# Another address for the second homes of the activation buffers, another order of the first modulation chunks, and the output of the LRU on other engines

## The chip, the cores and the metric

The kernel runs on one core of a Trainium2 chip. The time is the device time of one execution in microseconds; lower is better. One execution on the same kind of chip was recorded with the profiler, and all rows below are from it. PE is TensorE (PEld its weight loads), DVE is VectorE, ACT is ScalarE, POOL is GpSimd, SP is SyncE, which only issues DMAs here. "Granted clock" is the share of TensorE's full clock of 2.4 GHz that the chip granted; the other level, 0.50, is 1.2 GHz.

## What is computed

Two blocks of two layers each, on 256 tokens of width 1024 (and, in the first layer alone, 256 context tokens beside them). Cut to what matters here:

```
x_lat, x_ctx = layer_norm(x), layer_norm(ctx)
for l in 0, 1:                                 # first block
    sh1, sc1, g1, sh2, sc2, g2 = split(silu(c) @ w_mod[l] + b_mod[l], 6)
    a = x * (1 + sc1) + sh1                    # sh1: columns 0..1023, sc1: 1024..2047
    m = mixer(a)                               # a @ w_in, Fourier mix, two attentions, gates, w_out
    x = layer_norm(ALPHA * x + (1 + g1) * m)
    x = layer_norm(ALPHA * x + (1 + g2) * swiglu(x * (1 + sc2) + sh2))
for i in 0, 1:                                 # second block
    h = modulate(rms_norm(x), sh, sc)
    i == 0: y = (rg_lru(conv(h @ w_in)) * gelu(h @ w_y)) @ w_out + b_out
            # rg_lru: h[t] = a[t] * h[t-1] + u[t], a scan over the tokens
    i == 1: y = pool_mixer(h)
    x = x + gate * y
    x = x + gate * (relu(h @ w1) ** 2 @ w2)    # the MLP, width 4096
return rms_norm(x)
```

## The kernel before

Everything is float32. Activations lie transposed: 128 features on the partitions, 8 tiles of features, tokens along the row. A **unit** is a product with 512 columns of weights (4 output tiles `m`, 8 inner tiles `k`). Each float32 factor is split in a high part, rounded to the matmul's format, and a low rest, and a tile product is three matmuls, high x high (L546), high x low (L547) and low x high (L548), each with its own load of 128x128 weights on PEld. A unit's weights come by DMA into the buffers `RAW`; ACT copies them to the high part `SH` (L501) and DVE subtracts to get the low part `SL` (L507), one instruction of each for each `m`, mostly while the unit before is multiplied. The loop `Unit.pe` waits for `SL` of its `m`, for the bank of PSUM, and for its input tile by tile.

**Homes.** The moving operand of these matmuls is one of three pairs of buffers: `AB` (inputs of a layer), `HH`/`HL` (hidden values), `YB` (branch values). `pair` gives `AB` and `YB` two homes in the same memory: `at(0)` begins at a multiple of 128 bytes, `at(SHIFT)` begins `SHIFT` floats further on, and `H_IN` does so for `HH` and `HL`. `SHIFT` is 48 floats, 192 bytes, so the second home begins 64 bytes behind a multiple of 128 bytes. The first home serves layer 0, in which the matmuls take 512 tokens; the second serves layer 1 and the second block, in which all but a few take 256. `Y8H` and `Y8L`, the input of the LRU's output product, lie in the second home too. The weights `SH` and `SL` and all tile steps are multiples of 128 bytes.

**Modulation chunks.** `w_mod` is read in chunks of 512 columns. Most are hosted by a unit: `Side.pe_rows` (L367) multiplies the chunk by the conditioning vectors, DVE flips the result (`flip`), four small matmuls gather it (`gather_flipped`, L324), and DVE adds the bias (`dve`). The first four chunks belong to `Opening`: two of them are the shifts of layer 0 (tiles 0 to 3, then 4 to 7), two the scales. `Opening.sp` issues XIN, the first unit's weights and then the four chunks, all on SP's queue, into `SIDE`, `EARLY1` (in the high half of `AB`), `EARLY2` (in the low half) and `EARLY3` (in `YB`). `Opening.pe` runs `rows_of` (L1769) and `turn` for all four, one behind another; `Opening.dve` has the matching `flip` (L1702) and `add` (L1707) between the statistics, the reciprocal (L1723), the splits of the first unit's weights and the centring of tiles 0 and 1 (L1033, L1067), and then makes the scales in `DER` (`prep`, L2150). Then `Norm` runs: for each tile, ACT writes X (L1091) and the modulated tile (L1110), DVE rounds it into the high part of `AB` (L1052) and subtracts for the low (L1054), and PE starts the first unit (`w_in`, by tiles: all four `m` of tile 0, then of tile 1, and so on).

**LRU.** Two units `gelu[0]`, `gelu[1]` (`w_y`) are multiplied while DVE makes the scans. `GeluLru.dve` has, in this order: the splits of `gelu[1]`'s weights 0 and 1, `scan` of tiles 0 to 3, the splits 2 and 3, `scan` of tiles 4 to 7 (GI times LT at L676, then four scans at L679). `LruOut.pool` multiplies each tile by its gate on POOL (L1818), `LruOut.dve` waits for that, rounds (L1825) and subtracts (L1827) tile by tile. The splits of `lru_w_out` come between the two halves. The unit behind, a `Residual` with `late=4`, takes input tiles 0 to 3 of its first two `m` first, then tiles 4 to 7 of them.

Of the kernel before, what the change touches and what calls it, by code (L numbers as in the profile page):

```python
# [25 lines left out]
P = 128  # L26
# [20 lines left out]
SHIFT = 48  # L47
# [77 lines left out]
class Counts:  # L125
# [30 lines left out]
    def up(self, name, by=1):  # L156
# [13 lines left out]
            "tap_done", "tile_squared"],  # L170
    "dve": ["weight_low", "dve_read", "side_summed", "side_flipped", "side_added", "dve_done", "centred", "input_low", "one_minus_a2", "scanned",
            "max_done", "probs_ready", "branch_low", "keys_copied", "hidden_low", "var_done",
            "rotary_copied", "rotated_done", "lambda_done", "diagonals", "bias_done", "latent_normed", "copied_out"],
# [7 lines left out]
def build(nc, A, out, const):  # L181
# [42 lines left out]
    def reg(name, at, shape, dt=F32):  # L224
# [43 lines left out]
    EARLY1, EARLY2, EARLY3 = (sb(f"EARLY{j + 1}", [P, KT, 512], at=at)  # L268
                              for j, at in enumerate((AH_AT, AL_AT, YH_AT)))
# [58 lines left out]
    class Side:  # L328
# [3 lines left out]
        flip_at = 3  # L332

# [36 lines left out]
        def flip(self, e, K, j):  # L370
            e.wait_ge(sem["side_rows"], K.at("side_rows", j + 1))
            e.transpose(MODROW[:, :], PS[4][:, :]).then_inc(K.up("side_flipped"), 1)
# [7 lines left out]
        def dve(self, e, K, j):  # L380
            e.wait_ge(sem["side_turned"], K.at("side_turned", j + 1))
# [65 lines left out]
    class Unit:  # L447
# [3 lines left out]
        mid = None  # L451
        kt = KT
# [50 lines left out]
        def split_dve(self, e, K, m):  # L503
            p = m // 2
            e.wait_ge(sem["weight_high"], K.at("weight_high", m + 1))
# [17 lines left out]
        def pe(self, e, K):  # L523
            waited = -1
            for m, k in self.order():
                if self.side and self.by_k and (m, k) == (0, self.rows_at):
                    self.side.pe_rows(e, K, 0)
# [117 lines left out]

    class GeluLru(Gelu):
# [25 lines left out]
        def scan(self, e, K, half):  # L672
            t = slice(4 * half, 4 * half + 4)
            e.wait_ge(sem["root_done"], K.at("root_done", 4 * half + 4))
            e.wait_ge(sem["gated_done"], K.at("gated_done", 4 * half + 4))
            e.tensor_tensor(GI[:, t, :], GI[:, t, :], LT[:, t, :], ALU.mult).then_inc(K.up("dve_done"), 1)  # L676
            e.wait_ge(sem["dve_done"], K.own("dve_done"))
            for k in range(4 * half, 4 * half + 4):
                e.tensor_tensor_scan(XC[:, k, :], LA[:, k, :], GI[:, k, :], 0.0, ALU.mult, ALU.add) \  # L679
                    .then_inc(K.up("scanned"), 1)  # L680

        def dve(self, e, K):
# [9 lines left out]
            self.scan(e, K, 0)  # L692
            for m in (2, 3):
                self.nxt.split_dve(e, K, m)
            self.scan(e, K, 1)
# [204 lines left out]
    class Norm:  # L900


# [133 lines left out]
        def dve(self, e, K):  # L1036
# [9 lines left out]
            for k in range(KT):  # L1046
                if k + 1 < KT and (k or not self.split):
                    self.centre(e, K, k + 1)
                if self.to == "a":
# [5 lines left out]
                        .then_inc(K.up("input_low"), 1)  # L1055

# [550 lines left out]
    class Opening:  # L1607
# [3 lines left out]
        ROWS = (4, 3)  # L1611
# [3 lines left out]
        def __init__(self, unit, norm):  # L1615
            self.unit, self.norm = unit, norm
            unit.loaded = True

# [6 lines left out]
        def sp(self, e, K):  # L1625
# [7 lines left out]
            for j in range(4):  # L1633
                e.dma_start(self.places[j][:, :, :], rows(wmod[0])[:, :, j * 512:(j + 1) * 512]) \
                    .then_inc(K.up(f"chunk{j}_loaded", 16), 16)
# [28 lines left out]
        def dve(self, e, K):  # L1664
# [32 lines left out]
            name, first = bmod[0]  # L1697
            t, r = place[name]

            def flip(j):  # L1700
                e.wait_ge(sem["side_rows"], K.at("side_rows", j + 1))
# [741 lines left out]
```

## Time and profile before

| | |
|---|---|
| median of 3 runs | 2149.03 us (2142.33 to 2150.68) |
| the profiled execution's own time | 2156.49 us |
| its span, first to last instruction | 2154.3 us |
| mean granted clock | 0.959 |
| PE busy | 1993.8 us, 93% |
| PEld busy | 1644.9 us, 76% |
| DVE busy | 1285.3 us, 60% |
| ACT busy | 845.8 us, 39% |
| POOL busy | 138.9 us, 6% |
| bytes read from HBM | 329.31 MB, 153 GB/s over the span |

A busy PE is not PE at its peak: a matmul's record reaches over the next one's start, so the pace is read from the starts, or from how many start in a window, not from the busy share. The layers follow each other in time: layer 0 to about 1045 us, layer 1 to 1635, the LRU layer with its MLP to 1931, and pooling with its MLP to the end.

### The profile page before, as it was taken

How to read it: one execution, taken by the hardware profiler on the slowest of the kernel's cores; microseconds unless marked ns; L12 is line 12 of the kernel's file. 1: busy time of each engine (PE TensorE's matmuls, PEld its weight loads, DVE VectorE, ACT ScalarE, POOL GpSimd, SP SyncE). 2: the span in 40 equal slices, each digit the busy share in tenths (PEclk: the TensorE clock that was granted, in tenths of full speed). 3: DMA queues.
4: the chain of work that ended last, by engine and by line, in shares of the span. 5: the costliest groups of instructions: out<-in, count | busy, mean ns of one | idle time of the engine just before them, and what ended most of it. 6: DMA issues, size and time to landing. Idle time of an engine off the chain costs nothing.

```text
span 2154.3 us, 32049 instructions
## 1 busy us (share of the span) xinstructions
PE 1993.8 (93%) x12468; PEld 1644.9 (76%) x12468; DVE 1285.3 (60%) x2184; ACT 845.8 (39%) x1364; POOL 138.9 (6%) x118
## 2 busy tenths in 40 slices
PE   4999989999999999999898989989997899988998
PEld 2776657546768788887677664879997899988998
DVE  5422464564447567777634466566667776676665
ACT  4422263263124122222433444354445644444444
POOL 0000000000030001203000000020111300000000
PEclk8999999999999999999899899999997999998999
DMA  8642513105544555546465140856652446543653
GB/s 292 215 139 78 176 40 93 49 1 186 166 159 144 189 193 195 196 156 227 120 213 172 49 133 1 274 196 196 196 195 91 145 157 191 182 155 98 196 186 127
DMA packets 280758, 332.07 MB, mean 154 GB/s; under 512 B 13190, under 2 KB 229692, under 8 KB 280508
## 3 DMA queue, kind: packets, MB, share of 16 engines
q1 hardware_dynamic: 268608, 323.05, 46.0%
q10 hardware_dynamic: 12028, 7.32, 1.3%
q8 instruction: 85, 1.39, 0.3%
q14 instruction: 37, 0.30, 0.0%
HBM read 329.31 MB, written 1.05 MB: 153 GB/s over the span
## 4 chain that ended last, share of the span: by engine, by line
PE 75%; DVE 8%; issue 5%; DMA 5%; ACT 4%; POOL 1%; SPq 1%; DVEq 0%; ACTq 0%; POOLq 0%
PE ps L546 20%; PE ps L547 19%; PE ps L548 19%; PE ps L1316 3%; DVE SL L507 2%; PE ps L1342 2%; DMA RAW<-in_w_in 2%; PE ps L367 2%; PE ps L1326 2%; PE ps L924 1%; ACT SH L501 1%; DMA RAW<-in_w_out 1%; DMA EARLY<-in_w_mod 1%; PE ps L1551 1%; DMA RAW<-in_w_branch 1%
## 5 line engine op out<-in xcount | busy, mean ns | idle before, releaser
L507 DVE TENSOR_TENSOR SL<-RAW,SH 128x1024 fp32r<-128x1024 f32 (+2 forms) x448 | 524.8, 1175 | 434.6 <-ACT SH L501 429.9
L546 PE MATMUL ps<-AB,SH 128*128 128x256 f32 (+1 forms) x1984 | 646.7, 326 | 38.8 <-DVE AB L1054 20.7
L547 PE MATMUL ps<-AB,SH 128*128 128x256 f32 (+1 forms) x1984 | 639.7, 322 | 0.0
L548 PE MATMUL ps<-AB,SL 128*128 128x256 f32 (+1 forms) x1984 | 639.0, 322 | 0.0
L501 ACT ACTIVATE SH<-RAW 128x1024 fp32r<-128x1024 f32 (+2 forms) x448 | 443.2, 997 | 439.4 <-PE ps L548 273.7
L546 PEld LDWEIGHTS ps<-AB,SH 128*128 128x128 f32 x1984 | 379.7, 191 | 90.1 <-issue 32.2
L548 PEld LDWEIGHTS ps<-AB,SL 128*128 128x128 f32 x1984 | 379.7, 191 | 29.4
L547 PEld LDWEIGHTS ps<-AB,SH 128*128 128x128 f32 x1984 | 379.2, 191 | 28.0
L546 PE MATMUL ps<-HH,SH 128*128 128x256 f32 (+1 forms) x992 | 307.0, 309 | 4.0 <-DVE HL L757 1.6
L547 PE MATMUL ps<-HL,SH 128*128 128x256 f32 (+1 forms) x992 | 304.7, 307 | 0.0
L548 PE MATMUL ps<-HH,SL 128*128 128x256 f32 (+1 forms) x992 | 304.6, 307 | 0.0
L546 PEld LDWEIGHTS ps<-HH,SH 128*128 128x128 f32 x992 | 188.0, 189 | 19.5 <-issue 4.2
L548 PEld LDWEIGHTS ps<-HH,SL 128*128 128x128 f32 x992 | 187.9, 189 | 9.8
L547 PEld LDWEIGHTS ps<-HL,SH 128*128 128x128 f32 x992 | 187.0, 189 | 9.3
L771 POOL TENSOR_TENSOR S<-X 128x512 f32<-128x512 f32 (+1 forms) x6 | 10.7, 1780 | 1462.3 <-DVE X L798 1462.3
L546 PE MATMUL ps<-YB,SH 128*128 128x256 f32 (+1 forms) x256 | 84.8, 331 | 9.1 <-DVE SL L507 6.1
L1376 ACT ACTIVATE PR<-ps,SM 128x512 f32<-128x512 f32 (+1 forms) x96 | 59.2, 616 | 62.2 <-PE ps L1326 55.8
L547 PE MATMUL ps<-YB,SH 128*128 128x256 f32 (+1 forms) x256 | 83.1, 324 | 0.0
L548 PE MATMUL ps<-YB,SL 128*128 128x256 f32 (+1 forms) x256 | 82.9, 324 | 0.0
L777 POOL TENSOR_TENSOR S<-S,SQR 128x256 f32<-128x256 f32 (+1 forms) x51 | 52.0, 1020 | 445.6 <-ACT SQR L827 445.6
L798 DVE SCALAR_TENSOR_TENSOR X<-ps,DER,X 128x256 f32<-128x256 f32 x96 | 43.1, 477 | 60.8 <-PE ps L548 60.7
L415 DVE SCALAR_TENSOR_TENSOR MODROW<-SIDE,CC,MODROW 128x512 f32<-128x512 f32 x98 | 77.5, 790 | 3.0
(283 smaller groups left out, 2188.1 us busy)
## 6 DMA issues: line engine op xcount, KB each, us to landing
SIDE<-in_w_mod SPq DMA_DIRECT2D x45, 2048.0 KB, 8.0
RAW<-in_ffn_w SPq DMA_DIRECT2D x64, 1024.0 KB, 5.4
RAW<-in_w_in SPq DMA_DIRECT2D x44, 1024.0 KB, 6.1
RAW<-in_w_ffn_gate SPq DMA_DIRECT2D x22, 1024.0 KB, 8.6
RAW<-in_w_ffn_up SPq DMA_DIRECT2D x22, 1024.0 KB, 5.4
RAW<-in_w_ffn_down SPq DMA_DIRECT2D x16, 1024.0 KB, 5.6
RAW<-in_w_branch SPq DMA_DIRECT2D x24, 512.0 KB, 3.6
RAW<-in_w_out SPq DMA_DIRECT2D x8, 1024.0 KB, 6.4
```

The costliest lines, as they stand in the source:

```text
L367: ins = e.matmul(PS[4][32 * g:32 * g + 32, :], CC[:, k, :], SIDE[:, k, :], start=k < 4, stop=k >= 4)
L415: e.scalar_tensor_tensor(out=MODROW[:, :], in0=SIDE[:, k, :], scalar=v, in1=MODROW[:, :], op0=ALU.mult, op1=ALU.add).then_inc(K.up("side_s ...
L501: e.activation(SH[:, m, 0:kt, :], RAW[p][:, 0:kt, o:o + P], ACT.Copy).then_inc(K.up("weight_high"), 1)
L507: e.tensor_tensor(SL[:, m, 0:kt, :], RAW[p][:, 0:kt, o:o + P], SH[:, m, 0:kt, :].bitcast(F32), ALU.subtract).then_inc(K.up("weight_low"), 1)
L546: e.matmul(ps, SH[:, m, k, :], xh, start=k == 0, stop=False)
L547: e.matmul(ps, SH[:, m, k, :], xl, start=False, stop=False)
L548: ins = e.matmul(ps, SL[:, m, k, :], xh, start=False, stop=k == self.kt - 1)
L777: e.tensor_tensor(S2[:, c0:c1], S2[:, c0:c1], SQR[:, t % 2, c0:c1], ALU.add).then_inc(K.up("square_added"), 1)
L798: ins = e.scalar_tensor_tensor(out=X[:, i, c:c + SEQ], in0=PS[m][:, c:c + SEQ], scalar=self.scale(s, i), in1=X[:, i, c:c + SEQ], op0=ALU.m ...
L1316: e.matmul(self.scores_of(n), q, k, start=True, stop=True).then_inc(K.up("scores_done"), 1)
L1326: ins = e.transpose(PS[self.TURNED[n % 2]][:, j * P:(j + 1) * P], PR[:, n % 2, j * P:(j + 1) * P], IDENT)
L1376: e.activation(PR[:, n % 2, 0:c1 - c0], self.scores_of(n), ACT.Exp, bias=SM[:, n % 4:n % 4 + 1], accum_out=SM[:, 4 + n % 4:5 + n % 4]).the ...
```

## The change

There are three edits. `SHIFT` becomes 56 floats, so the second homes of `AB`, `YB`, `HH` and `HL` begin 224 bytes on, 96 bytes behind a multiple of 128. The four chunks of the opening are fetched and used in the order 1, 3, 2, 4 (by first column 0, 1024, 512, 1536), the last two of them inside the first unit and its normalization; the third chunk goes to another place (`EARLY2` now in the region of the hidden buffers), the sums use bank 7 in place of bank 3. And the LRU's output is made with whole halves (128x1024) on DVE and ACT, not tile by tile on POOL and DVE, with the second scan behind `gelu[1]`'s first part.

```diff
-SHIFT = 48
+SHIFT = 56
...
-    EARLY1, EARLY2, EARLY3 = (sb(f"EARLY{j + 1}", [P, KT, 512], at=at)
-                              for j, at in enumerate((AH_AT, AL_AT, YH_AT)))
+    EARLY1, EARLY3 = (sb(f"EARLY{j}", [P, KT, 512], at=at) for j, at in ((1, AH_AT), (3, YH_AT)))
+    EARLY2 = reg("EARLY2", 2048, [P, KT, 512])
...
+    def gated_out(e, K, half):
+        t = slice(4 * half, 4 * half + 4)
+        e.tensor_tensor(XC[:, t, :], XC[:, t, :], GB[:, t, :], ALU.mult).then_inc(K.up("gated_out"), 1)
+
+    def low_out(e, K, half):
+        t = slice(4 * half, 4 * half + 4)
+        e.wait_ge(sem["out_high"], K.at("out_high", 1))
+        e.tensor_tensor(Y8L[:, t, :], XC[:, t, :], Y8H[:, t, :].bitcast(F32), ALU.subtract) \
+            .then_inc(K.up("hidden_low", 4), 4)
+
+    def high_out(e, K, half):
+        t = slice(4 * half, 4 * half + 4)
+        e.wait_ge(sem["gated_out"], K.at("gated_out", 1 - half))
+        e.activation(Y8H[:, t, :], XC[:, t, :], ACT.Copy).then_inc(K.up("out_high"), 1)
...
-        ROWS = (4, 3)
+        ROWS = (4, 7)
+        CHUNKS = (0, 2, 1, 3)
...
-            flip(0)
+            self.flip(e, K, 0)
             self.unit.split_dve(e, K, 0)
-            add(0)
+            self.unit.split_dve(e, K, 1)
+            self.flip(e, K, 1)
+            self.add(e, K, 0)
             e.wait_ge(sem["root_done"], K.at("root_done", 1))
             e.reciprocal(RSTD[:, :], VAR[:, :]).then_inc(K.up("dve_done"), 1)
-            flip(1)
-            self.unit.split_dve(e, K, 1)
-            add(1)
-            self.unit.split_dve(e, K, 2)
+            self.add(e, K, 1)
+            self.prep(e, K, 0)
             e.wait_ge(sem["dve_done"], K.own("dve_done"))
             self.norm.centre(e, K, 0)
-            flip(2)
+            self.unit.split_dve(e, K, 2)
             self.norm.centre(e, K, 1)
-            add(2)
-            flip(3)
-            add(3)
-            self.norm.prep(e, K)
-            self.unit.split_dve(e, K, 3)
...
+        def dve_between(self, e, K, k):
+            if k == 0:
+                self.unit.split_dve(e, K, 3, 4)
+                self.flip(e, K, 2)
+            if k == 1:
+                self.add(e, K, 2)
+                self.flip(e, K, 3)
+            if k == 2:
+                self.add(e, K, 3)
+                self.prep(e, K, 1)
...
+        def pe_between(self, e, K, m, k):
+            if (m, k) == (0, 1):
+                self.turn(e, K, 2)
+                self.rows_of(e, K, 3)
+            if (m, k) == (2, 1):
+                self.turn(e, K, 3)
...
-            rows_of(0)
-            for j in range(4):
-                if j < 3:
-                    rows_of(j + 1)
-                turn(j)
+            self.rows_of(e, K, 0)
+            self.rows_of(e, K, 1)
+            self.turn(e, K, 0)
+            self.turn(e, K, 1)
+            self.rows_of(e, K, 2)
...
+    class GeluOut(Gelu):
+        def act(self, e, K):
+            high_out(e, K, 0)
+            super().act(e, K)
+
+        def dve(self, e, K):
+            e.wait_ge(sem["products"], K.at("products"))
+            e.wait_ge(sem["act_read"], K.at("act_read"))
+            gated_out(e, K, 0)
...
+            e.tensor_tensor(GI[:, t, :], GI[:, t, :], LT[:, t, :], ALU.mult).then_inc(K.up("dve_done"), 1)
+            low_out(e, K, 0)
+            for m in (0, 1):
+                self.nxt.split_dve(e, K, m)
...
+            for k in range(4, 8):
+                e.tensor_tensor_scan(XC[:, k, :], LA[:, k, :], GI[:, k, :], 0.0, ALU.mult, ALU.add) \
+                    .then_inc(K.up("scanned"), 1)
...
+            gated_out(e, K, 1)
+            for m in (2, 3):
+                self.nxt.split_dve(e, K, m)
...
-    seq += [LruBias(), conv[0], conv[1], Gates(), gelu[0], LruOut(0, 4), gelu[1], LruOut(1, 8)]
+    seq += [LruBias(), conv[0], conv[1], Gates(), gelu[0], gelu[1], LruOut()]
```

`Norm.dve` calls `dve_between` behind each tile `k`, and `Unit.pe` calls `pe_between` ahead of each step `(m, k)`, for the first unit alone.

On PE in the opening, before: the sums of four chunks stand ahead of the first unit. `EARLY_98`, `_99` and `_100` are EARLY1, EARLY2 and EARLY3's buffers in the kernel before.

```order
L1769 MATMUL ps<-SIDE,CC 32x512 x8
L1769 MATMUL ps<-EARLY_98,CC 32x512 x8
L324 MATMUL ps<-MODROW,CON 32x12 x4
L1769 MATMUL ps<-EARLY_99,CC 32x512 x8
L324 MATMUL ps<-MODROW,CON 32x12 x4
L1769 MATMUL ps<-EARLY_100,CC 32x512 x8
L324 MATMUL ps<-MODROW,CON 32x12 x8
L546 MATMUL ps<-AB,SH 128x512
```

Now, in the same place (here `EARLY_100` is the third chunk's buffer and `EARLY_99` the fourth's):

```order
L1793 MATMUL ps<-SIDE,CC 32x512 x8
L1793 MATMUL ps<-EARLY_98,CC 32x512 x8
L324 MATMUL ps<-MODROW,CON 32x12 x8
L1793 MATMUL ps<-EARLY_100,CC 32x512 x8
L550 MATMUL ps<-AB,SH 128x512
```

And 12 matmuls of the first unit later on PE, in the changed kernel:

```order
L552 MATMUL ps<-AB,SL 128x512
L324 MATMUL ps<-MODROW,CON 32x12 x4
L1793 MATMUL ps<-EARLY_99,CC 32x512 x8
L550 MATMUL ps<-AB,SH 128x512
L551 MATMUL ps<-AB,SH 128x512
```

The fourth chunk's sums and the turns of the third and fourth have moved from ahead of the first unit to behind its first tile.

On DVE at the LRU's output, before: the second scan and the first half's rounding (four such pairs stand there) come ahead of the splits of `lru_w_out`. The scans are named SCALAR_TENSOR_TENSOR here and TENSOR_TENSOR_SCAN in the trace.

```order
L679 SCALAR_TENSOR_TENSOR XC<-LA,GI 128x256 x4
L507 TENSOR_TENSOR SL<-RAW_54,SH 128x1024 x2
L676 TENSOR_TENSOR GI<-GI,LT 128x1024
L679 SCALAR_TENSOR_TENSOR XC<-LA,GI 128x256 x4
L1825 CAST YB<-XC 128x256
L1827 TENSOR_TENSOR YB<-XC,YB 128x256
```

Now:

```order
L701 SCALAR_TENSOR_TENSOR XC<-LA,GI 128x256 x4
L509 TENSOR_TENSOR SL<-RAW_54,SH 128x1024 x2
L653 TENSOR_TENSOR XC<-XC,GB 128x1024
L1874 TENSOR_TENSOR GI<-GI,LT 128x1024
L659 TENSOR_TENSOR YB<-XC,YB 128x1024
L509 TENSOR_TENSOR SL<-RAW_53,SH 128x1024 x2
L1880 SCALAR_TENSOR_TENSOR XC<-LA,GI 128x256 x4
L653 TENSOR_TENSOR XC<-XC,GB 128x1024
L509 TENSOR_TENSOR SL<-RAW_54,SH 128x1024 x2
L659 TENSOR_TENSOR YB<-XC,YB 128x1024
```

The first two splits of `lru_w_out` now stand ahead of the second scan, the products with the gates are DVE's, and the last instruction ahead of the output product is the second half's low part.

## Rows read from the trace of the kernel before

**Rows 1.** The page, part 4: the chain that ended last, by engine.
```profile
PE 75%; DVE 8%; issue 5%; DMA 5%; ACT 4%; POOL 1%; SPq 1%; DVEq 0%; ACTq 0%; POOLq 0%
```

**Rows 2.** Busy time by window: the header, then layer 1's FFN and the first MLP.
```profile
core 0: us, PE busy (x) PEld busy (x) DVE busy (x) ACT busy (x) POOL busy (x), PEclk, DMA share, GB/s
1460.00:1560.00 100.00, 100.00 (x885) 100.00 (x884) 66.77 (x94) 44.74 (x57) 10.48 (x12) 1.00 0.64 203
1780.00:1880.00 100.00, 100.00 (x851) 100.00 (x850) 69.79 (x105) 42.05 (x52) 0.00 (x0) 1.00 0.60 189
```

**Rows 3.** The same view, over the two stretches of the MLPs without a gap.
```profile
1748.00:1931.00 183.00, 181.11 (x1528) 180.39 (x1527) 126.58 (x202) 77.51 (x107) 3.71 (x5) 0.99 0.56 175
1991.00:2148.00 157.00, 157.00 (x1337) 157.00 (x1336) 104.26 (x157) 67.79 (x93) 3.70 (x5) 1.00 0.54 169
```

**Rows 4.** Groups by line and form at 1056 to 1074, 660 to 690, 126 to 131.
```profile
L547 PE MATMUL ps<-AB,SH 128*128 128x512 f32 x24 | 9.5, 396 | 0.0
...
L547 PE MATMUL ps<-AB,SH 128*128 128x512 f32 x44 | 17.1, 389 | 0.0
...
L717 PE MATMUL ps<-SL,AB 128*128 128x256 f32 x14 | 4.0, 283 | 0.0
```

**Rows 5.** Timeline of PE behind side rows: start us, us long, instruction.
```profile
1089.20 1.47 PE L367 MATMUL ps<-SIDE,CC 128*32 128x512 f32 x12
...
1090.83 0.28 PE L547 MATMUL ps<-AB,SH 128*128 128x256 f32 x1
...
1091.89 0.28 PE L547 MATMUL ps<-AB,SH 128*128 128x256 f32 x1
```

**Rows 6.** Timeline of PE in the values of layer 0, first home.
```profile
127.07 0.28 PE L717 MATMUL ps<-SL,AB 128*128 128x256 f32 x1
...
128.51 0.28 PE L717 MATMUL ps<-SL,AB 128*128 128x256 f32 x1
```

**Rows 7.** Timeline of the opening, PE, DVE and ACT; in brackets the idle time before.
```profile
30.23 1.92 PE L1769 MATMUL ps<-EARLY,CC 128*32 128x512 f32 x16 [1.94 <-DMA EARLY<-in_w_mod]
...
32.40 3.34 DVE L1723 RECIPROCAL RSTD<-VAR 128x512 f32<-128x512 f32 x1
...
36.85 2.94 PE L1769 MATMUL ps<-EARLY,CC 128*32 128x512 f32 x16 [4.65 <-DMA EARLY<-in_w_mod]
...
41.87 0.69 DVE L1067 TENSOR_TENSOR NT<-NT,RSTD 128x512 f32<-128x512 f32 x1
...
42.01 3.64 PE L1769 MATMUL ps<-EARLY,CC 128*32 128x512 f32 x16 [2.14 <-DMA EARLY<-in_w_mod]
...
47.58 1.09 ACT L1110 ACTIVATE A<-X,MODT,DER 128x256 f32<-128x256 f32 x2 [4.16 <-DVE DER L2150]
...
50.07 0.77 PE L546 MATMUL ps<-AB,SH 128*128 128x512 f32 x1 [3.11 <-DVE AB L1054]
```

**Rows 8.** Busy time by window where the first unit starts.
```profile
50.00:55.00 5.00, 4.93 (x12) 3.95 (x13) 4.86 (x9) 3.63 (x7) 0.00 (x0) 0.53 1.07 380
```

**Rows 9.** Timeline of DVE, scan and output of the LRU.
```profile
1695.15 2.43 DVE L679 TENSOR_TENSOR_SCAN XC<-LA,GI 128x256 f32<-128x256 f32 x4
1697.51 2.88 DVE L507 TENSOR_TENSOR SL<-RAW,SH 128x1024 fp32r<-128x1024 f32 x2
...
1702.10 4.35 DVE L679 TENSOR_TENSOR_SCAN XC<-LA,GI 128x256 f32<-128x256 f32 x4
1706.37 0.75 DVE L1825 CAST YB<-XC 128x256 fp32r<-128x256 f32 x1
...
1709.98 2.35 DVE L507 TENSOR_TENSOR SL<-RAW,SH 128x1024 fp32r<-128x1024 f32 x2
```

**Rows 10.** Timeline of POOL beside them.
```profile
1697.76 10.04 POOL L1818 TENSOR_TENSOR XC<-XC,GB 128x256 f32<-128x256 f32 x8 [10.94 <-ACT GB L643]
```

**Rows 11.** PE restarting for `lru_w_out`: its timeline, and the window behind.
```profile
1711.25 0.58 PE L546 MATMUL ps<-YB,SH 128*128 128x256 f32 x1 [5.58 <-DVE SL L507]
...
1711.00:1717.00 6.00, 5.75 (x27) 5.75 (x28) 5.86 (x12) 0.00 (x0) 0.00 (x0) 0.50 0.60 192
```

More of the change, by code:

```diff
@@ L451, in build @@
         mid = None
+        opening = None
         kt = KT
@@ L1617, in __init__ @@
             unit.loaded = True
+            unit.opening = norm.opening = self
+            unit.side.rows_ahead, unit.side.turns_ahead = 1, 2
         def vectors(self, e, K, names, signal):
@@ new lines, in add, with prep @@
+        def add(self, e, K, i):
+            e.wait_ge(sem["side_turned"], i + 1)
+            name, first = bmod[0]
+            t, r = place[name]
+            q = 4 * self.CHUNKS[i]
+            bias = VEC[:, t, r + first + q:r + first + q + 4].unsqueeze(2).to_broadcast([P, 4, 3])
+            e.tensor_tensor(MODT[:, 0, q:q + 4, :], PS[5][:, 0:12].rearrange("p (q v) -> p q v", v=3), bias,
+                            ALU.add).then_inc(K.up("side_added"), 1)
+        def prep(self, e, K, half):
+            t = slice(4 * half, 4 * half + 4)
+            e.wait_ge(sem["side_added"], K.own("side_added"))
+            for s in range(2):
+                e.tensor_scalar(DER[:, 2 + s, t], mod(0, 1, s)[:, t], 1.0, 1.0 / ALPHA, ALU.add, ALU.mult) \
+                    .then_inc(K.up("dve_done"), 1)
@@ new lines, in dve_between, with rows_of @@
+        def dve_between(self, e, K, k):
[8 more added lines that the diff above has]
+                self.prep(e, K, 1)
+        def rows_of(self, e, K, i):
+            e.wait_ge(sem[f"chunk{i}_loaded"], 16)
+            if i == 1:
+                e.wait_ge(sem["var_done"], K.at("var_done", 1))
+            if i >= 2:
+                e.wait_ge(sem["side_flipped"], i - 1)
+            for k in range(KT):
+                g = k % 4
+                ins = e.matmul(PS[self.ROWS[i % 2]][32 * g:32 * g + 32, :], CC[:, k, :], self.places[i][:, k, :],
+                               start=k < 4, stop=k >= 4)
+            ins.then_inc(K.up("side_rows"), 1)
@@ L1802, in build @@
     class LruOut:
-        def __init__(self, half, products):
-            self.tiles = range(4 * half, 4 * half + 4)
-            self.half, self.products = half, products
         def sp(self, e, K):
             pass
-        pe = act = sp
-        def pool(self, e, K):
-            for j, k in enumerate(self.tiles):
-                e.wait_ge(sem["scanned"], K.at("scanned", k - 7))
-                e.wait_ge(sem["act_read"], K.at("act_read", j - 3))
-                e.tensor_tensor(XC[:, k, :], XC[:, k, :], GB[:, k, :], ALU.mult).then_inc(K.up("gated_done"), 1)
@@ L1820, in dve @@
-        def dve(self, e, K):
-            e.wait_ge(sem["products"], K.at("products", -self.products))
-            for j, k in enumerate(self.tiles):
-                e.wait_ge(sem["gated_done"], K.at("gated_done", j + 1))
-                e.tensor_copy(Y8H[:, k, :], XC[:, k, :]).then_inc(K.up("dve_done"), 1)
-                e.wait_ge(sem["dve_done"], K.own("dve_done"))
-                e.tensor_tensor(Y8L[:, k, :], XC[:, k, :], Y8H[:, k, :].bitcast(F32), ALU.subtract) \
-                    .then_inc(K.up("hidden_low"), 1)
+        pe = pool = sp
```

92 lines of the change are left out of this document (47 added, 45 removed).

## The prediction, made before the result was known

> **What bounds the kernel now.** I read the chain of work that ended last first: 75% of the span is PE, no other engine has over 8% [rows 1]. So the pace of the matmuls sets the time, and beside it the places where PE starts late. The windows come second, because a busy PE says nothing of its pace. Over 100 us of layer 1's FFN, at the full granted clock, 885 matmuls start; over 100 us of the first MLP, at the same clock, with the same engine never idle, the same shapes and the same two buffers in their second homes, only 851 [rows 2]. Both counts include about two that began earlier. The pace is 113.3 ns in the one and 117.8 ns in the other (from the starts in the timeline), 4.5 ns or 4% apart.
>
> What tells them apart is neither the code nor the address. The timeline shows that a stream takes one of the two paces within some ten matmuls of a break and keeps it until the next break. Behind the side rows L367 it takes the slow one: from 1090.83 to 1091.89 are nine matmuls, 117.8 ns each [rows 5], and so behind the other side rows of layer 1. Layer 1's FFN keeps the fast one over 1483 matmuls, both MLPs the slow one over about 1300 each. So something fetched for a matmul collides with something else in one phase and not in the other.
>
> The address does matter. With 512 tokens a matmul lasts 389 ns in the first home, and 396 ns in the second, the weights lying at the same places [rows 4]; between starts that is 226.7 and 233.3 ns. With 256 moving columns and everything at a multiple of 128 bytes, the one stream there is, the values of layer 0, runs 12 matmuls in 1.44 us, 120.0 ns each [rows 6], 283 ns long [rows 4]. So the trace holds four cases: offset 0 with 512 columns, no loss; offset 0 with 256, 120.0; offset 64 with 512, 233.3; offset 64 with 256, 113.3 or 117.8. Offset 96 is in none of them.
>
> **Part 1, the address.** It adds and removes no instruction. DVE and ACT write the same sizes; nothing in the trace suggests that they care. What it may change is the pace. The pool to be won is the slow streams. The two MLP stretches hold 1528 + 1337 = 2865 starts [rows 3], of which about 50 are not of these streams: 2815 x 4.5 ns = 12.7 us. In layer 1 and the LRU I count by the starts 590 more at the slow pace, in pieces of 22 to 118 like that of [rows 5]: 2.6 us. The 140 matmuls with 512 tokens in the second home lose 6.6 ns each [rows 4]: 0.9 us. Together 16.2 us to win. To lose: the 2953 matmuls now at the fast pace, at 4.5 ns, are 13.3 us; if all 6355 went to the 120.0 ns of [rows 6], 2953 x 6.7 + 3402 x 2.2 = 27.3 us.
>
> Which? Half of a 64-byte step would be a new relation between the two fetches (data and weights) rather than a repetition of one that is there. At offset 64 a stream free of loss already exists and is stable over 1483 matmuls; at 0 the one 256-column stream has found none. I take it that moving further from 0 keeps the free phase and makes the lossy one rarer. It is a choice, not a derivation: with steps of 64 bytes in two of the trace's cases I can't exclude that a row of 1024 bytes that begins half-way in a step needs one more fetch for each matmul.
>
> The Trainium skill speaks against this part. "SBUF — State Buffer", section "Who interferes with whom", gives PE two read ports, one for the moving operand and one for the weights, and calls them independent; the section "Door 1" has lines of 16 bytes, of which both 64 and 96 are multiples. By that page no home differs from another and the sum for part 1 is 0. The 389 against 396 ns of [rows 4] disagree with it, so I hold it as a rival and not as the forecast.
>
> **Part 2, the opening.** Before, ACT's first modulated tile begins at 47.58 after 4.16 us of waiting for the scales, which DVE makes behind the fourth chunk, and PE starts the first unit at 50.07 [rows 7]. The shifts and scales of tiles 0 to 3 now need the first two chunks only, and the second has landed at 30.2 (PE's sums start at 30.23 behind that DMA [rows 7]). Path on DVE: the flip and one more split (1.2) now stand ahead of the reciprocal, which takes 3.34 and so ends near 36.9 in place of 35.7; small adds and scales 0.4; centring twice 0.69 to 38.7; then ACT's X 0.8 and modulated tile 1.09 to 40.8, under which DVE does a split and the next centring (to 41.3); rounding and low part 1.1. PE can start at about 42.5, 7.6 us sooner.
>
> Given back: the fourth chunk's sums, 1.92 at the full clock (3.64 at half [rows 7]), now lie in PE's stream behind tile 0, with two turns of 0.3 and three restarts: 2.8 us. DVE waits there for PE, first for the third turn, then to flip the fourth chunk; queued behind are the centring of tile 3 and the low part of tile 2, which by my schedule end near 53.1, when PE, which is at tile 1 until about 53, asks for tile 2. That costs 0.2. The half clock is paid in both: 12 matmuls in 5 us at 0.53 [rows 8]. Sum: 7.6 - 2.8 - 0.2 = 4.6 us won. Bounds: 2 if DVE's wait is 2.5 us worse than scheduled, 6 if the restarts are free. SP's queue gains too: the next side chunk waits for three sums, not four. Nothing behind it stands at an absolute time: PE is never starved until 150 us.
>
> **Part 3, the LRU.** Before, PE idles 5.58 us to 1711.25 for the first split of `lru_w_out`, and then runs at clock 0.50: 27 starts in 6 us [rows 11]. DVE is late because the second scan (4.35, against 2.43 for the first) and the rounding (0.75 against 0.29) run beside POOL's eight products [rows 9, 10]. Without POOL: scan to 1697.6, splits 2.35 (was 2.88) to 1699.9, gate product and GI x LT 1.2 each to 1702.3, first low part to 1703.6, behind ACT's rounding; split 0 to 1704.9, split 1 to 1706.3, scan 2.43 to 1708.7, gate product 1709.9, splits 2 and 3 to 1712.2, second low part 1713.4. PE ends `gelu[1]` near 1705.7 and goes on at once with 24 matmuls on tiles 0 to 3, 2.7 us, to 1708.4; then it waits 5.0 us for the second low part. Before, it had 96 matmuls left at 1711.25; now 72 at 1713.4, again at half clock for the first 27. That is 2.2 us later with 24 x 0.113 = 2.7 us less to do: 0.5 us won. If a shorter wait kept the clock up, 27 x 0.1 = 2.7 more; if ACT, which now rounds before it reads the `gelu[1]` banks, holds PE, up to 1.5 lost.
>
> **Sum.** 16.2 + 4.6 + 0.5 = 21.3 us. Against the profiled execution's own 2156.5 that is 2135.2. Against the median, 2149.0, 7.5 lower, it would be 2127.7. The 8 us between the lowest run and the median, and as much to the profiled one, are about what one long stream at the other pace is worth (1300 x 4.5 ns = 5.9 us); if that is the cause, the median has less of the pool left and the own time is the right base; if recording costs the 7.5, the median is. Between them, nearer the first: 2133.
>
> **Rivals.**
> *The mix stays.* The phases are set anew at each break, and about half stay slow. Parts 2 and 3 alone: 2149.0 - 5.1 = 2144. For it: the two long slow streams start behind a cold clock or a late DVE, which the address doesn't touch. Against it: the 6.6 ns of [rows 4]. The page above ends here too.
> *The collision becomes the rule.* At 96 bytes every 256-column matmul collides: 13.3 us more at 117.8 ns, less the 5.1: 2157, and 2171 at 120.0. For it: 512 columns at 64 bytes always collide, 256 at 0 always; only one of four cases has a free phase besides a lossy one. It decides the sign when 1130 (5.1 us / 4.5 ns) of the 2953 fast matmuls turn slow; one long stream does.
> *The opening gives nothing*, because PE waits for DVE, which waits for PE, at tiles 1 and 2: 4.6 less won, 2138 with the forecast's part 1.
>
> **Chances.** Streams all or nearly all fast 0.42 (2127 to 2138); mix stays, or is a bit better or worse, 0.30 (2139 to 2150); the collision the rule 0.22 (2155 to 2171), of which the 120.0 ns is 0.06; opening without gain, with the first, 0.06. The likeliest one's own range is 2127 to 2139. For 8 in 10 the range goes to the 2160s: 2127 to 2161. A measurement tells about 0.5%, 10.7 us, from no change: under 2138.3 is faster (0.42 and half of 0.06, and a few hundredths of a better mix: 0.47), over 2159.8 slower (two thirds of 0.22 and a tail: 0.18), the rest 0.35.
>
> **What would show it.** Right: over 100 us of either MLP about 885 starts and matmuls of 276 ns; no 117.8 behind side rows; the 512-token matmuls of layer 1 at 389. PE's first unit at 42.5 +- 1, the fourth chunk's sums 5 us later, under 0.5 us of idle ahead of tile 2. No POOL in the LRU behind 1690 us, scans at 2.43 throughout, PE idle 5 us in the middle of the first output unit and not ahead of it. Wrong: a third pace in the windows, above all 120 or more; or 851 starts in the MLPs as now.

## The result, and the profile after

The changed kernel takes 2156.94 us (median of 11 runs, 2151.69 to 2162.34) against 2149.03 (11 runs, 2142.33 to 2158.69): a ratio of 1.004, with 95% between 1.0023 and 1.0057. It is slower by 7.9 us, inside the 0.5% that I called no change, but clearly on the other side of the 2133 forecast. It is the time of the rival "the collision becomes the rule", 2157.

The bound is the same. The page of the changed kernel, part 4 (the chain by engine) and part 1 (busy us), beside [rows 1]:

```profile
PE 77%; DVE 8%; issue 5%; DMA 4%; ACT 4%; POOL 1%; SPq 1%; ACTq 0%; DVEq 0%; POOLq 0%
...
PE 2003.8 (93%) x12468; PEld 1658.4 (77%) x12468; DVE 1282.6 (60%) x2174; ACT 847.4 (39%) x1366; POOL 128.5 (6%) x110
```

PE is busy for 10 us more with the same matmuls. Busy time by window of the changed kernel, to be read as [rows 2]: layer 1's FFN, the first MLP, and the second MLP.

```profile
1460.00:1560.00 100.00, 100.00 (x848) 100.00 (x846) 63.70 (x84) 44.25 (x57) 10.50 (x12) 1.00 0.62 195
1780.00:1880.00 100.00, 100.00 (x848) 100.00 (x847) 68.80 (x103) 42.32 (x52) 0.00 (x0) 1.00 0.60 187
2020.00:2120.00 100.00, 100.00 (x847) 100.00 (x846) 70.90 (x110) 42.75 (x55) 0.00 (x0) 1.00 0.58 182
```

The full clock, PE without a gap, and 847 or 848 starts everywhere: the stretch that had 885 has lost 37, and the ones that had 851 have lost 3 or 4. The pace is 118.3 ns in every stream, and the intervals between starts are no longer even (115 to 123 ns in a repeating pattern). The clean pace of 113.3 ns occurs nowhere. The groups by line and form of that window say it in one row; before, the same row reads 276 ns:

```profile
L551 PE MATMUL ps<-AB,SH 128*128 128x256 f32 x180 | 50.6, 281 | 0.0
```

**The opening** went as scheduled. Timeline of the changed kernel, to be read against [rows 7]:

```profile
33.15 3.33 DVE L1740 RECIPROCAL RSTD<-VAR 128x512 f32<-128x512 f32 x1
...
41.73 0.69 DVE L1077 TENSOR_TENSOR AB<-A,AB 128x512 fp32r<-128x512 f32 x1
...
42.57 0.76 PE L550 MATMUL ps<-AB,SH 128*128 128x512 f32 x1 [3.26 <-DVE AB L1077]
...
47.14 1.90 PE L1793 MATMUL ps<-EARLY,CC 128*32 128x512 f32 x16
...
49.11 0.72 DVE L1753 STREAM_TRANSPOSE MODROW<-ps 128x512 f32<-128x512 f32 x1 [1.56 <-PE ps L1793]
```

The first unit starts at 42.57 in place of 50.07, and the fourth chunk's sums stand at 47.14 behind the first tile.

**The LRU** too. Timeline of DVE and PE there, against [rows 9] and [rows 11], and the window of PE's restart:

```profile
1692.92 2.44 DVE L701 TENSOR_TENSOR_SCAN XC<-LA,GI 128x256 f32<-128x256 f32 x4
...
1703.78 2.43 DVE L1880 TENSOR_TENSOR_SCAN XC<-LA,GI 128x256 f32<-128x256 f32 x4
...
1709.66 1.22 DVE L659 TENSOR_TENSOR YB<-XC,YB 128x1024 fp32r<-128x1024 f32 x1
...
1710.93 0.39 PE L550 MATMUL ps<-YB,SH 128*128 128x256 f32 x1 [4.28 <-DVE YB L659]
...
1706.00:1712.00 6.00, 1.72 (x13) 1.51 (x12) 4.85 (x5) 1.06 (x1) 0.00 (x0) 0.97 0.55 187
```

Without POOL beside it the second scan takes 2.43 us, not 4.35, and PE idles 4.28 us in the middle of the output's first unit and no longer 5.58 ahead of it.

**The two recorded executions by themselves mislead.** The one of after took 2154.33 us, the one of before 2156.49, though the medians stand 7.9 the other way. One reason is at layer 1's attention, which nothing in the change touches. The same window, first of before, then of after:

```profile
1165.00:1205.00 40.00, 36.15 (x168) 21.28 (x168) 27.36 (x58) 18.53 (x38) 0.00 (x0) 0.74 0.30 92
```

```profile
1165.00:1205.00 40.00, 33.17 (x177) 18.95 (x176) 32.73 (x74) 23.88 (x52) 0.00 (x0) 0.91 0.26 79
```

Behind the same pauses the half clock lasted 20.5 us in the one and 6.8 in the other, worth about 6 us. Of the eleven other recorded executions five have 6.8 to 10.2 us of it at this place and six 17.1 to 20.5, in no order of the edits. Laid one on the other, matmul by matmul, after is ahead by 5.3 us from the opening on, and by 9.9 where layer 1's FFN begins, at 1444 us of before's time (with the luck at the attention). Layer 1's FFN, 1483 matmuls at 118.3 where before had 113.3, takes 7 us of that back (3.0 ahead at 1634), the LRU adds 1.6 to the lead, and the MLPs and what lies about them take 3.2 from it, so that 1.4 are left. Had the recorded execution of before not had both MLPs at 117.8 and the long half clock, the loss would have stood in the traces as well.

### The profile page after: what moved, and what is told of

Read it like the earlier page. It is cut to its first block, busy times and chain, and to the rows that moved or that the text cites. A ratio compares the mean times of both kernels' runs of the same rounds, so it can differ in the third digit from the quotient of the medians.

```text
span 2152.5 us, 32028 instructions
## 1 busy us (share of the span) xinstructions
PE 2003.8 (93%) x12468; PEld 1658.4 (77%) x12468; DVE 1282.6 (60%) x2174; ACT 847.4 (39%) x1366; POOL 128.5 (6%) x110
## 4 chain that ended last, share of the span: by engine, by line
PE 77%; DVE 8%; issue 5%; DMA 4%; ACT 4%; POOL 1%; SPq 1%; ACTq 0%; DVEq 0%; POOLq 0%
PE ps L550 20%; PE ps L551 20%; PE ps L552 20%; PE ps L1341 3%; PE ps L1367 2%; DVE SL L509 2%; PE ps L368 2%; DMA RAW<-in_w_in 2%; PE ps L1351 2%; PE ps L947 1%; ACT SH L503 1%; DMA RAW<-in_w_out 1%; PE ps L1576 1%; DMA EARLY<-in_w_mod 1%; PE ps L1004 1%
## 5 line engine op out<-in xcount | busy, mean ns | idle before, releaser
L793 POOL TENSOR_TENSOR S<-X 128x512 f32<-128x512 f32 (+1 forms) x6 | 10.7, 1778 | 1458.9 <-DVE X L820 1458.9
L631 ACT ACTIVATE GATE<-ps 128x512 f32<-128x512 f32 (+1 forms) x48 | 23.4, 488 | 145.2 <-PE ps L552 145.2
```

## Experiments

Open were three things: whether it is the address alone that costs, whether the opening and the LRU gained what they should, and what about the address counts. For the last I had these theories: the operand's **own** address (modulo 128 bytes, as the prediction took it), a collision of rows with steps of **64** bytes, and the **distance** between where the moving operand and where the weights begin. `at(0)`, `SH` and `SL` all begin at the same place modulo 256 bytes, so the distance is 4 x `SHIFT` bytes in a second home, modulo 256, and 0 in a first. Before's is 192, after's 224.

The experiments are called e1 to e11 in the order in which they stand below; the last of their sections has e10 and e11. Times are medians with their range and number of runs; a ratio is to the kernel before on the same chip. Its median was 2148.4 beside the first four kernels (22 runs, 2130.8 to 2159.2), 2150.5 beside the next four (13 runs) and 2137.4 beside the last three (3 runs, 2131.9 to 2141.6). "Starts" are those within the windows 1460 to 1560, 1780 to 1880 and 2020 to 2120, as in [rows 2]; before's third is 851.

### The changed kernel with the homes left where they were

```diff
-SHIFT = 56
+SHIFT = 48
```

> The changed kernel with the second homes back at 64 bytes behind a multiple of 128 (SHIFT = 48), the opening and the LRU as changed. Theory A, the address sets the pace: streams of 256-column matmuls take 113.3 or 117.8 ns again, the uneven pace of 118.2 is gone, layer 1's FFN holds about 885 starts in 100 us, and the time is some 5 to 7 us under the kernel before, about 2143, ratio near 0.997. Theory B, the new opening and LRU moved the phases and the address is innocent: 848 starts in every window as in the changed kernel, and a time near 2156.

Measured: 2138.94 (2128.10 to 2148.41, 10 runs), ratio 0.9968 (0.9943 to 0.9992). Busy time by window, the three stretches:

```profile
1460.00:1560.00 100.00, 100.00 (x885) 100.00 (x884) 67.52 (x89) 46.10 (x59) 10.49 (x12) 1.00 0.60 196
1780.00:1880.00 100.00, 100.00 (x852) 100.00 (x851) 71.25 (x109) 42.31 (x55) 0.00 (x0) 1.00 0.59 188
2020.00:2120.00 100.00, 100.00 (x886) 100.00 (x885) 67.08 (x102) 45.45 (x66) 3.70 (x5) 1.00 0.52 165
```

The pace of 113.3 ns is back in the FFN, and this time the second MLP has it too, with instructions that differ from before's in nothing there. The one number is worth 15.5 us by the ratios (1.0040 less 0.9968, of 2149) and 18.0 by the medians. This kernel beats both by the medians.

### The kernel before with the new address alone

```diff
-SHIFT = 48
+SHIFT = 56
```

> The kernel before with SHIFT = 56 alone. Theory A: every 256-column stream in the second homes runs at about 118.2 ns, 848 starts in 100 us in layer 1's FFN and in both MLPs; the time is that of the changed kernel plus the 5 to 7 us of the opening and the LRU: about 2162, ratio 1.005 to 1.007. Theory B: two paces as in the kernel before, ratio 1.000.

Measured: 2162.65 (2157.52 to 2167.74, 6 runs), ratio 1.0066 (1.0041 to 1.0092): 14.2 us (8.8 to 19.8). The window of the FFN:

```profile
1460.00:1560.00 100.00, 100.00 (x847) 100.00 (x846) 64.41 (x89) 42.66 (x54) 10.51 (x12) 1.00 0.58 189
```

The address costs the same from either side. It isn't something that the new opening or the LRU brings about.

### The new opening alone

The kernel before with the changed `Opening`, `dve_between` and `pe_between`, and neither the address nor the LRU's edits:

```diff
-        ROWS = (4, 3)
+        ROWS = (4, 7)
+        CHUNKS = (0, 2, 1, 3)
...
```

> The new opening alone: SHIFT = 48 and the LRU's output as before. Both theories: first matmul of the first unit at 42.6, 5.3 us won by 125 us and kept through layer 0; PE idle 5.6 us ahead of the output product in the LRU. Theory A: two paces of 113.3 and 117.8 behind 1080 us, time about 2145, ratio 0.997 to 0.999. Theory B, if it is the opening that moved the phases: 118.2 everywhere.

Measured: 2142.40 (2129.90 to 2152.55, 10 runs), ratio 0.997 (0.9941 to 0.9999): 6.4 us. PE's timeline at the opening and at the LRU's output:

```profile
42.56 0.77 PE L550 MATMUL ps<-AB,SH 128*128 128x512 f32 x1 [3.81 <-DVE AB L1077]
...
1697.76 0.58 PE L550 MATMUL ps<-YB,SH 128*128 128x256 f32 x1 [6.58 <-DVE SL L509]
```

The first unit starts where it does in after, and the lead over before is 5.0 us at 114 us. But it isn't kept through layer 0, as I had expected: at 331 us it is 1.2. Behind a pause near 255 us, where the instructions are those of before, the half clock lasted longer in this execution. The same window, before, then this kernel:

```profile
240.00:330.00 90.00, 81.01 (x417) 50.06 (x416) 53.48 (x134) 44.59 (x115) 0.00 (x0) 0.96 0.27 90
...
240.00:330.00 90.00, 81.66 (x387) 48.83 (x386) 52.32 (x131) 43.58 (x114) 0.00 (x0) 0.89 0.20 66
```

The LRU still waits ahead of `lru_w_out`. The lead of e1 over this one grows by about 1 us across that place (5.3 to 5.5 us ahead of the second `gelu` unit, 6.5 behind the restart), which is the LRU's part read from these two traces. The medians are 3.5 apart, which their spread of 20 us doesn't tell from 1.

### The second home at 128 bytes

```diff
-SHIFT = 56
+SHIFT = 32
```

> The changed kernel with the second homes at a multiple of 128 bytes (SHIFT = 32). Theory A in the form that the offset to the weights, which lie at multiples of 128, decides: 120.0 ns for every 256-column stream, as the values of layer 0 had, 835 starts in 100 us, and 226.7 ns for 512 columns in layer 1 in place of 233; about 10 us over the changed kernel, 2167. Theory B: no difference from the changed kernel, 848 starts.

Measured: 2161.58 (2157.11 to 2163.39, 5 runs), ratio 1.0063 (1.0040 to 1.0087); starts 835, 845, 836.

```profile
1460.00:1560.00 100.00, 100.00 (x835) 100.00 (x834) 63.77 (x84) 43.32 (x55) 10.51 (x12) 1.00 0.58 192
```

```profile
L551 PE MATMUL ps<-AB,SH 128*128 128x512 f32 x23 | 9.1, 395 | 0.0
```

The second row is the group of layer 1's 512-token matmuls, of the same kernel. If the offset modulo 128 decided, this home would be a first home: 389 ns with 512 columns. It is 395. So "a multiple of 128" is not what makes the first home what it is. The expected 835 starts everywhere were missed too: the first MLP has 845. This home also has two paces, 120.0 and 118.7 ns in its long streams.

### The weights moved by 64 bytes, the homes left

The changed kernel with `SHIFT = 48`, and:

```diff
+    offset[0] += 64
     SH = sb("SH", ...)
```

This moves `SH`, `SL` and all that lies behind them (`RAW`, `SIDE`, `YB`, `HH`, `HL` and more) by 64 bytes, and not `AB`. So `AB`'s distance to the weights becomes 128 in its second home and 192 in its first, and the others keep theirs, at addresses that are all new.

> The changed kernel with SHIFT = 48 and 64 bytes left free ahead of SH, so that SH, SL and everything behind them (YB, HH, HL too) lie 64 bytes further on, and AB alone stays. AB's second home then is 128 bytes (modulo 256) from the weights, HH's and HL's still 192. Theory C, the distance between the moving operand and the weights decides: matmuls on AB in layer 1's FFN and in the MLPs run as with SHIFT = 32, at 119.3 ns on average, those on HH and HL at 113.3 or 117.8. Theory D, the moving operand's own address decides: AB at 113.3 or 117.8, and HH and HL, now at a multiple of 256, at another pace.

Measured: 2173.18 (2 runs, 2170.57 and 2175.80), ratio 1.0138 (1.0104 to 1.0173). Groups by line and form of the first MLP, 1800 to 1900, then of layer 0, 660 to 690 (line numbers are one higher than after's):

```profile
L552 PE MATMUL ps<-HL,SH 128*128 128x256 f32 x159 | 44.1, 277 | 0.0
...
L553 PE MATMUL ps<-AB,SL 128*128 128x256 f32 x128 | 36.2, 283 | 0.0
...
L552 PE MATMUL ps<-AB,SH 128*128 128x512 f32 x43 | 17.0, 395 | 0.0
```

In one stretch the units that read `HL`, which was moved together with the weights, keep the two paces of 192 (113.4 ns in most of them, 117.8 in one), and those that read `AB`, which was not moved at all, have got the uneven pace (118.9 ns between starts). And layer 0's `AB`, at the address at which it took 389 ns [rows 4], takes 395. An operand's own address explains none of it; its distance to the weights explains all three rows. The intervals between starts say it once more. With 512 tokens in layer 1, `AB` at the distance 128 here repeats 229, 238, 229, 237, 230, 237 ns, as in the kernel with the second home at 128 bytes above, whose `AB` is as far from the weights but lies elsewhere; in layer 0, now at 192, it takes 236 and 231 ns in turn, as layer 1 does in the kernel before the change.

Layer 0's `AB` costs 2016 matmuls at 6.6 ns, 13 us. That is not all that makes this kernel the slowest: in the recorded execution the half clock near 255 us also cost 9 us more than in after's (granted clock 0.83 in this window, 0.96 there).

```profile
240.00:330.00 90.00, 81.64 (x376) 47.93 (x369) 52.66 (x133) 43.13 (x113) 0.00 (x0) 0.83 0.23 76
```

`RAW` and `SIDE`, into which the DMAs write, have moved with the weights, so what the reading of `AB` collides with could also be the DMAs' writes. The end of the changed kernel speaks against it: without any DMA traffic PE starts 44 matmuls in 5 us, as many as with it (848 in 100). Busy time by window:

```profile
2130.00:2135.00 5.00, 5.00 (x44) 5.00 (x44) 2.95 (x4) 2.52 (x4) 1.48 (x2) 1.00 0.00 0
2135.00:2140.00 5.00, 5.00 (x44) 5.00 (x43) 1.22 (x3) 2.84 (x7) 1.48 (x2) 1.00 0.00 0
```

What ACT and DVE read and write beside the matmuls was not separated by a run; they are busy in bursts, while a stream's pattern doesn't change.

### The second home at 256 bytes

```diff
-SHIFT = 56
+SHIFT = 64
```

> The changed kernel with SHIFT = 64: second homes 256 bytes behind the first, which is the distance of the first homes again if 256 bytes are the period. The matmuls with 512 columns tell it: 226.7 ns in layer 0 in the first home, but 233.1 to 233.4 in layer 1 with SHIFT = 32, 48 and 56 alike. Period of 256 bytes: 226.7 here. Otherwise it is something of layer 1 and not the home: 233.3 again. For 256 columns both leave it open; by the values of layer 0, 120.0.

Measured: 2164.07 (2 runs), ratio 1.0096 (1.0060 to 1.0132); starts 835, 835, 836. The FFN's window, and the group of layer 1's 512-token matmuls:

```profile
1460.00:1560.00 100.00, 100.00 (x835) 100.00 (x834) 62.94 (x84) 43.26 (x55) 10.50 (x12) 1.00 0.60 189
```

```profile
L551 PE MATMUL ps<-AB,SH 128*128 128x512 f32 x23 | 8.9, 389 | 0.0
```

At 256 bytes the second home is a first home again: 389 ns with 512 columns, and with 256 columns a steady 120.0 ns, that of [rows 6]. So the period is 256 bytes. The two sizes want opposite things: of the distances tried, 0 is the best for 512 columns and the worst for 256.

### The second home at 64 bytes

```diff
-SHIFT = 56
+SHIFT = 16
```

> The changed kernel with SHIFT = 16: also 64 bytes behind a multiple of 128, but 64 and not 192 bytes from the weights modulo 256. If only the place modulo 128 counts: 113.3 or 117.8 in each stream, as with SHIFT = 48, mean 114.8 to 115.8. If the place modulo 256 counts: one pace of its own, likely over 118.

Measured: 2151.80 (2147.36 to 2160.27, 8 runs), ratio 1.0031 (0.9997 to 1.0065); starts 851, 851, 852.

```profile
1460.00:1560.00 100.00, 100.00 (x851) 100.00 (x851) 64.22 (x84) 43.83 (x56) 10.52 (x12) 1.00 0.61 193
```

Modulo 128 this is before's home; yet all but three short streams (48 to 93 matmuls) run at 117.8 ns, the FFN too. I had expected a pace over 118 for the case that the place modulo 256 counts, and it is a little under. It is a second way to see that 128 isn't the period, and that 64 and 192 differ: the distance has a sign.

### The second home at 160 bytes

```diff
-SHIFT = 56
+SHIFT = 40
```

> The changed kernel with SHIFT = 40, 160 bytes, 32 behind a multiple of 128. If half a step of 64 bytes is what costs the clean pace: one uneven pace near 118.3 for every stream, as with SHIFT = 56, 848 starts in 100 us. If the distance modulo 256 grows worse steadily towards 128: between 118.3 and 119.3.

Measured: 2158.51 (2152.81 to 2164.25, 6 runs), ratio 1.0043 (1.0013 to 1.0074); starts 855, 854, 845. The long streams have one of two uneven paces, 117.3 and 118.7 ns, 117.8 on average. Neither of the two expectations has a pace under 118.3. 32 bytes on the other side of 192 cost about what they cost on this side.

### The first experiment's kernel again, in another execution

> The same kernel as e1_home64, recorded once more. If a stream's pace is set anew in each execution by the phase at a break: the three long streams (layer 1's FFN, the two MLPs) need not have the paces of e1_home64 (885, 852 and 886 starts in 100 us); the time lies between 2128 and 2149, lower by 5.9 us for each long stream at 113.3. If the program alone sets it: the same three counts.

Measured: 2139.13 (one run; before beside it 2131.88 to 2141.61).

```profile
1460.00:1560.00 100.00, 100.00 (x885) 100.00 (x884) 66.03 (x90) 45.83 (x58) 10.48 (x12) 1.00 0.63 198
1780.00:1880.00 100.00, 100.00 (x885) 100.00 (x884) 74.08 (x114) 44.81 (x57) 0.00 (x0) 1.00 0.63 198
2020.00:2120.00 100.00, 100.00 (x852) 100.00 (x851) 70.07 (x104) 43.45 (x55) 1.48 (x2) 1.00 0.57 179
```

The same instructions at the same addresses, and the first MLP has changed from 852 starts to 885, the second from 886 to 852. So at a distance of 192 the pace of a stream isn't fixed by the program. The two recordings were made on two chips, so this alone could be the chip's doing. Against it stands e3, recorded on the same chip as e1 and with the same instructions in the second MLP: it has 851 starts there where e1 has 886. I take the pace to be drawn anew in each execution; two recordings of one kernel on one chip, which would show it, were not made.

### The second home at 176 and at 208 bytes

```diff
-SHIFT = 56
+SHIFT = 44
```

> The changed kernel with SHIFT = 44, second homes 176 bytes from the weights modulo 256, 16 bytes from the best so far. If a distance other than a multiple of 64 always costs: one uneven pace near 118. If the clean pace lives in a band around 192: some streams at 113.3, mean under 117.

Measured: 2162.63 (2 runs), ratio 1.0120 (1.0064 to 1.0177); starts 841, 841, 841.

```diff
-SHIFT = 56
+SHIFT = 52
```

> The changed kernel with SHIFT = 52, 208 bytes, 16 on the other side. The same two readings: one uneven pace near 118, or a band around 192 with streams at 113.3. Between 192 (two paces) and 224 (118.3 for all) the second is not excluded.

Measured: 2159.93 (2 runs), ratio 1.0108 (1.0051 to 1.0164); starts 842, 842, 842. Both ratios stand beside only three runs of before, which were low ones; against its 2149 they would be 1.006 and 1.005.

```profile
1460.00:1560.00 100.00, 100.00 (x841) 100.00 (x840) 63.86 (x88) 42.57 (x54) 10.53 (x12) 1.00 0.58 188
```

```profile
1460.00:1560.00 100.00, 100.00 (x842) 100.00 (x841) 64.08 (x88) 42.88 (x54) 10.48 (x12) 1.00 0.60 190
```

16 bytes to either side of 192 are enough to lose the clean pace (176 in the first row, 208 in the second). No neighbour is better than 192.

### The distances side by side

Mean time between starts, worked out from the starts in the timelines of the long streams of layer 1 and the second block (256 columns) and of layer 1's three stretches with 512 tokens:

| distance, bytes | 256 columns, ns | 512 columns, ns | kernel's median, us |
|---|---|---|---|
| 0 | 120.0, steady | 226.7 | 2164.1 |
| 64 | 117.8, steady; rarely 113.3 | 228.9 | 2151.8 |
| 128 | 118.7 or 120.0, uneven | 233.3 or 232.5 | 2161.6 |
| 160 | 117.3 or 118.7, uneven | 234.2 | 2158.5 |
| 176 | 119.3, uneven | 233.3 or 231.2 | 2162.6 |
| 192 | 113.3 or 117.8, steady | 233.3 | 2138.9 |
| 208 | 119.2, uneven | 234.6 or 230.2 | 2159.9 |
| 224 | 118.3, uneven | 233.3 | 2156.9 |

All rows have the new opening and LRU; the last row is the changed kernel, and the medians of 176 and 208 come from an occasion on which before had 2137.4. A stream has one of two paces at other distances too, but only at 192 is one of them 113.3 ns in about half of the streams. Before stood at the one distance of the eight at which half of the streams run free; the change moved away from it.

## Why the prediction was wrong

**What bounds the kernel: right.** The pace of the matmuls decides, the windows' counts show it, and the pace belongs to a stream. e9 bears out what I had read from one execution, and adds that the same program can come out with other paces. One reading was too strong: behind the side rows of layer 1 the pace is the slow one in six of nine streams, not in all; those from 1165, 1358 and 1431 us run at 113.4.

**Part 1: the step that failed is the choice** that "moving further from 0 keeps the free phase and makes the lossy one rarer". At 224 bytes there is no free phase: 118.3 ns in all streams. In place of 16.2 us won, the address costs 15.5 (e1 to after) or 14.2 (before to e2). The working behind it allowed this: 2953 fast matmuls of the recorded execution x (118.3 - 113.3) = 14.8 us, and 3402 slow ones x 0.5 = 1.7, together 16.5. The losing side of the sum was sized well ("13.3 us" at 117.8); only the sign was chosen wrongly.

Two readings led there. I ordered the four cases of the trace by offset modulo 128, as one line from 0 to 64 to 96, and read a trend from two points. The offset that the kernel calls 64 is a distance of 192 modulo 256, so the two points were 0 and 192, and the point beyond lay on the way back to 0, which is no smooth way either: 208 has 119.2 ns, 224 has 118.3. The trace did hold a warning: with 512 columns the second home was the worse one [rows 4], with 256 the better. A quantity that helps one shape and hurts the other isn't "further away is better", and from such rows nothing follows for a third value. The chances were also not those of that reading: with no mechanism, "the collision becomes the rule", 0.22, deserved at least as much as the 0.42 of its opposite. A single value at which streams run free is easier left than found.

The Trainium skill, "SBUF — State Buffer", section "Who interferes with whom", has the reads of the moving operand and of the weights independent of each other. The rows of e5 disagree: with `AB` left where it was and the weights moved, its 512-token matmuls go from 389 ns [rows 4] to 395, and in the first MLP the operand that moved with the weights has 277 ns and the one that didn't 283. The measurement decides: where one of the two begins, seen from the other, sets the pace. That it does so through their reads is my reading; no row shows a read.

**Part 2, the opening: right, to within what executions differ by.** PE starts at 42.57 (42.5 forecast), the fourth chunk's sums are at 47.14 (5 us later, forecast), and nothing idles ahead of tile 2. The term that was off is the half clock: I let 12 matmuls run at it, as in [rows 8]. In the changed kernel the clock rose behind seven. Busy time by window there:

```profile
42.50:46.00 3.50, 3.43 (x8) 2.78 (x9) 3.43 (x6) 0.98 (x3) 0.00 (x0) 0.51 1.05 406
46.00:49.00 3.00, 3.00 (x30) 1.08 (x29) 0.72 (x2) 1.43 (x3) 0.00 (x0) 1.00 1.08 357
```

5.3 us won by this trace, 6.4 (0.2 to 12.7) by e3's ratio, 4.6 forecast. The early rise is luck in part: e1, e3 and e9 have the same opening, the half clock lasted longer in them, and their leads over before at 114 us are 5.1, 5.0 and 4.4 us.

**Part 3, the LRU: right, about 1 us too small.** No POOL, scans of 2.43, an idle time in the middle of the unit of 4.28 (5.0 forecast). 1.6 us won (about 1 from e3 to e1) and 0.5 forecast. In after's trace the reason is the clock: I had the restart at half clock for as long as in [rows 11], and it stood at 0.97 in the window above, fell a little later and for fewer matmuls, so that 37 start in the first 6 us behind the pause against 27. In e1 and e9, with the same LRU, the half clock there lasted as long as before (6.8 us), so this too is of the execution and not of the edit.

**Parts 2 and 3 together: 6.9 us** by the traces, and 6.9 by e1's ratio (0.9968 of 2149); forecast 5.1. With the 14.2 of e2 the sum is +7.3; measured +7.9 by the medians. (The 15.5 can't test the sum: it was made from e1's ratio and the changed kernel's own.)

**The base between own time and median: not borne out.** I gave the 7.5 us between them to one long stream at the other pace or to the recording. The changed kernel has one pace in all its streams, and its eleven runs still lie 10.7 us apart, nearly in the order of their mean granted clock: 0.966 in the fastest, 0.959 in the slowest. e1 and e9 are two executions of one kernel, 2128.10 at a mean clock of 0.967 and 2139.13 at 0.960, with one MLP at the fast pace each and the long half clock at the attention in both. 0.7% of the clock over such a span is at most 15 us, enough for the 11 between them. So much of what single executions differ by comes with the granted clock, for which the prediction had no term. What decides how long the half clock lasts stays open.

**Rivals.** "The collision becomes the rule" is what happened: 2157 at 117.8 ns, measured 2156.9 at 118.3. (That it hits to 0.1 us is luck: 0.5 ns too little over 6355 matmuls, 3.2 us, and 1.8 us too little gained in parts 2 and 3 partly take each other away.) "The mix stays" is refuted by the windows, and "the opening gives nothing" by the traces of after and e3 and by e3's ratio.

## What is shown and what stays open

Shown: the address costs 14 to 16 us whether or not the other edits are there; it acts through the time between matmuls at full clock with PE never idle; and what counts is the distance between the moving operand and the weights (e5), modulo 256 bytes and not 128 (e4, e6, e7). Argued only: that the cause is a collision of two fetches in the memory, since no row names a wait within a matmul; and that a stream's pace is drawn in each execution and not given by the chip. Open: why 192 of all distances has so many streams at 113.3 ns; what at a break decides which pace a stream takes (behind side rows it is the slow one in 25 of 36 streams of the four recordings with 192, elsewhere in 38 of 133); and whether 512 columns have a better distance than 0. The LRU's edits alone, and a layout with 0 for the 512-token units and 192 for the others throughout, were not tried: before has the latter already but for 140 matmuls (0.9 us).

## What to carry to other kernels

When PE is never idle at full clock and the same shape still shows two counts in equal windows, the layout is a suspect: move one operand by 16, 32 and 64 bytes against the other before touching the schedule, try each shape by itself, and record the kernel twice, since neither a stream's pace nor the length of the half clock need come out the same again. A trend over addresses mustn't be read from two points, nor modulo a number that was never varied. And a change of several parts hides its best version: here the opening and the LRU alone win 0.3%, the address loses 0.7%, and together they looked like no change.

## What the runs showed of the hardware that I had not expected

- The distance modulo 256 bytes between the moving operand and the weights changes the pace of float32 matmuls with a weight load each by up to 6%: 113.3 to 120.0 ns with 256 columns, 226.7 to 234.6 with 512. No distance is best for both.
- 16 bytes decide: measured beside each other, the kernel takes 2139.1 us at 192 (one run), 2159.9 at 208 and 2162.6 at 176 (two runs each).
- At 192 bytes a stream of over 1000 matmuls holds one of two paces, 113.3 or 117.8 ns, and the same program had other paces in another execution, on another chip (852 and 886 starts, then 885 and 852).
- The half clock behind the same pause lasted 20.5 us in some executions and 6.8 in others, at layer 1's attention and in much the same way near 255 us in layer 0. The runs of one kernel, 10.7 us apart, lie nearly in the order of their mean granted clock, 0.966 in the fastest and 0.959 in the slowest.
